# Two transformer-like blocks on one core: each feed-forward down projection as seven half-sized products instead of one full product

## The reference

```python
# first block (in the kernel: phase E)
h = rms_norm(x, norm_ffn_pre)
f = (silu(h @ w_ffn_gate) * (h @ w_ffn_up)) @ w_ffn_down      # [1024, 2816] @ [2816, 1024]
x = x + rms_norm(f, norm_ffn_post)
# second block (phase H); conv: depthwise, causal, width 3
g = rmsnorm(h, norm_ffn_g) @ w_up                             # [1024, 5632]
a, b = split(conv(g) + conv_b)
h = h + (silu(b) * a) @ w_down                                # [1024, 2816] @ [2816, 1024]
return rmsnorm(h, norm_final_g)
```

## Time and profile before

| | us |
|---|---|
| median of 3 runs | 3183.2 |
| lowest, highest | 3179.53, 3187.27 |
| the profiled execution | 3176.86 |
| its span in the trace | 3175.2 |
| PE matmuls busy | 2987.9 (94% of the span) |
| VectorE busy | 1918.5 (60%) |
| ScalarE busy | 1225.2 (39%) |
| GpSimd busy | 514.5 (16%) |

### The profile page before, as it was taken

How to read it: one execution, slowest core, us unless ns; L and a number is a source line. 1 busy time by engine, 2 the same in 40 slices (tenths; PEclk the granted TensorE clock), 3 DMA queues, 4 the chain that set the end, 5 groups by cost and what they waited for, 6 DMA issues and landing times.

```text
span 3175.2 us, 40775 instructions
## 1 busy us (share of the span) xinstructions
PE 2987.9 (94%) x15215; PEld 2443.7 (77%) x15215; DVE 1918.5 (60%) x2600; ACT 1225.2 (39%) x1900; POOL 514.5 (16%) x481
## 2 busy tenths in 40 slices
PE   8989999999989898999999998999988899999997
PEld 6767778778877676888878877788867677777886
DVE  3546565575675538555546675555745777776667
ACT  3531441542542445333322224556645444443212
POOL 3211121221221302222220001233410000000000
PEclk9999999999999999999999999999989999999999
DMA  4255356265242642222223234333244444443233
GB/s 141 67 165 141 119 130 180 82 147 162 89 116 68 225 138 80 80 79 82 86 85 128 96 115 139 103 121 115 86 144 139 119 116 116 117 116 120 93 106 119
DMA packets 268750, 370.81 MB, mean 117 GB/s; under 512 B 13346, under 2 KB 208688, under 8 KB 266048
## 3 DMA queue, kind: packets, MB, share of 16 engines
q1 hardware_dynamic: 240576, 261.45, 26.2%
q0 software_dynamic: 22224, 90.62, 10.4%
q10 hardware_dynamic: 5808, 16.79, 1.8%
HBM read 285.92 MB, written 129.03 MB: 131 GB/s over the span
## 4 chain that ended last, share of the span: by engine, by line
PE 72%; DVE 13%; ACT 5%; DMA 5%; issue 3%; POOL 1%; SPq 0%; DVEq 0%; ACTq 0%
PE PS L661 20%; PE PS L367 19%; PE PS L2373 17%; PE PS L1479 2%; DVE gate_up L2269 1%; PE PS L1373 1%; PE PS L1445 1%; PE PS L2978 1%; PE PS L1362 1%; DMA down_raw<-up_sums 1%; DMA sb_branch<-u_scratch 1%; PE PS L2965 1%; DVE silu_out L2249 1%; ACT silu_out L2101 1%; DVE w_L L2222 1%
## 5 line engine op out<-in xcount | busy, mean ns | idle before, releaser
L661 PE MATMUL PS<-hH,w_H 128*128 128x512 f32 x1072 | 452.2, 422 | 25.9 <-DVE w_L L324 13.0
L661 PE MATMUL PS<-hH,w_L 128*128 128x512 f32 x1072 | 425.1, 397 | 0.0
L661 PE MATMUL PS<-hL,w_H 128*128 128x512 f32 x1072 | 423.0, 395 | 0.0
L2189 DVE TENSOR_TENSOR ffn_sum<-ffn_sum,PS 128x1024 f32<-128x1024 f32 x160 | 195.4, 1221 | 139.3 <-PE PS L367 139.2
L324 DVE TENSOR_TENSOR w_L<-w_raw,w_H 128x1024 fp32r<-128x1024 f32 x107 | 133.8, 1251 | 216.7 <-ACT w_H L319 216.5
L661 PEld LDWEIGHTS PS<-hH,w_H 128*128 128x128 f32 x1072 | 206.2, 192 | 71.4 <-issue 12.1
L661 PEld LDWEIGHTS PS<-hH,w_L 128*128 128x128 f32 x1072 | 204.1, 190 | 46.3
L661 PEld LDWEIGHTS PS<-hL,w_H 128*128 128x128 f32 x1072 | 205.7, 192 | 35.6 <-issue 1.7
L2373 PE MATMUL PS<-hH,fast_w 128*128 128x512 f32 x672 | 227.3, 399 | 4.0 <-DVE fast_w L2222 3.9
L2373 PE MATMUL PS<-sums,w_H 128*128 128x512 f32 x672 | 212.5, 398 | 9.1 <-DVE gate_up L2269 8.4
L367 PE MATMUL PS<-hH 128*128 128x512 f32 x960 | 219.8, 390 | 0.0
(11 more groups left out here) (462 smaller groups left out, 6421.4 us busy)
## 6 DMA issues: line engine op xcount, KB each, us to landing
up_sums<-in_w_up POOLq DMA_DIRECT2D x24, 1408.0 KB, 10.9
w_raw<-in_w_in SPq DMA_DIRECT2D x62, 512.0 KB, 4.4
u_scratch<-unit_staged SPq DMA_DIRECT2D x50, 512.5 KB, 4.9
hidden_scratch<-hidden SPq DMA_DIRECT2D x42, 512.0 KB, 4.7
down_raw<-up_sums SPq DMA_DIRECT2D x42, 512.0 KB, 6.7
gate_up<-hidden_scratch SPq DMA_DIRECT2D x20, 1024.0 KB, 4.9
w_raw<-in_w_up SPq DMA_DIRECT2D x23, 512.0 KB, 4.0
...
```

The lines of the kernel that those rows point to most:

```text
L661: mm = e.matmul(PS[:, f.bank(o, half), :], w[:, k0 + k, :], x[:, k, half * HALF:(half + 1) * HALF], start=(k == 0 and j == 0), stop=(k == ...
L2189: e.tensor_tensor(yacc[:, b, :], yacc[:, b, :], bank2(4 + 2 * (b % 2)), ALU.add).then_inc(added, 1)
```

## The change

The down projection of both phases becomes seven products of halves, as in Strassen's scheme (Winograd's form). The 1024 tokens are halved, the 22 tiles are halved (tiles 0 to 10 and 11 to 21), and the 1024 output columns are halved. A step n = 11 q + i is tile i of product q: a 128x512 operand from the hidden side (a half of a hidden tile, or one of four sums of a pair of tiles), a 128x512 operand from the weight side (a quarter of the weights, or one of four sums), split as before, and 4 blocks x 3 passes = 12 matmuls. A product is accumulated over its 11 steps in PSUM (products 0 and 1 in the same banks, 2 to 4, 5 and 6). Its sum is read out once, by ScalarE for products 0 and 1 (`act_taken`), by VectorE for the others (`dve_taken`), which combines it with the other sums.

- All operands are streamed from DRAM: 2 x 256 KB a step, in four raw slots in turn, and nine slots for split operands.
- The four hidden sums of a pair of tiles are made by GpSimd in the tile loop (`pair_sums`), from the tile just computed and one loaded back, and stored. VectorE (E) or ScalarE (H) waits for them before it overwrites the hidden tile.
- The weight sums of both phases are made by 2 x 16 more accumulating DMAs on GpSimd's queue. E's 16 come first, then the 32 of before, then H's 16. B issues 3 + 5 + 5 for each pair of heads and 3 for the last, F one after every third step.
- The `keep_busy` transposes ahead of the down projection go.
- Blocks 0 to 3 are complete after product 4. Their epilogue is put between steps 60 to 75, at fixed step numbers on each engine; that of blocks 4 to 7 comes after the last step, all stages of a block in a written order.
- Some semaphores are merged with others (`dve_steps_B`, `inverse_started`, `F_dve_steps`), and tiles are laid out anew in SBUF; the order of the work is the same there.

```diff
+        DOWN_E_PARTS, UP2_PARTS, DOWN_H_PARTS = 16, 32, 16
+        def weight_sum_parts(e):
+            def part(dst, src, add):
+                if part.n:
+                    e.wait_ge(sem("weights_summed"), 16 * part.n)
+                e.dma_start(dst, src, accum_op=ALU.add if add else ALU.bypass, max_dma_last_dim=2 * DFF)\
+                    .then_inc(sem("weights_summed"), 16)
+                part.n += 1
+            part.n = 0
+            def down(t, w):
+                rows, half = NG * P, NG * P // 2
+                b11, b12, b21, b22 = (w[r * rows:(r + 1) * rows, c * HALF:(c + 1) * HALF] for r in range(2) for c in range(2))
+                for n, src, add in ((0, b11, False), (2, b12, False), (0, b12, True), (2, b22, True),
+                                    (1, t[0], False), (1, b22, True), (3, t[1], False), (3, b21, True)):
+                    for i in range(2):
+                        blk = slice(i * half, (i + 1) * half)
+                        part(t[n][blk], src[blk], add)
+                        yield
...
+            yield from down(down_sums[0], a["w_ffn_down"][0])
+            yield from gate_up(up2_sums, a["w_up_2"][0])
+            yield from down(down_sums[1], a["w_down_2"][0])
...
-                    sums(2)
+                    sums(3)
...
-                sums(2 if p == LAST else 4)
+                    e.memset(t[:, :, :], 0.0).then_inc(sem("inverse_started"), 1)
+                sums(3 if p == LAST else 5)
...
-                sums(4)
+                sums(5)
...
+        DOWN_A = ((HIDDEN, 0, 0), (HIDDEN, NG, 0), (SUMS, 1), (SUMS, 0), (SUMS, 3), (SUMS, 2), (HIDDEN, NG, 1))
+        DOWN_B = ((DOWN, 0, 0), (DOWN, NG, 0), (TSUM, 1), (TSUM, 0), (DOWN, NG, 1), (TSUM, 2), (TSUM, 3))
+        DOWN_BANK, DOWN_FIRST = (4, 4, 0, 0, 0, 4, 4), (0, 2, 5)
...
+        NSLOT = len(OP_SLOTS)
+        slot_no = lambda n: {ND - 2: 5, ND - 1: 6}.get(n, n % NSLOT)
...
+        raw_of = lambda n: RAW_SLOTS[n if n < 5 else 5 + (n - 5) % 4]
+        evac_after = lambda q: NG * q + NG - 1 + NSLOT - 1
...
+        def down_load(e, tag, n, w_down):
+            q, i = n // NG, n % NG
+            if n < 2:
+                e.wait_ge(sem("fast_L"), since(tag, "fast_L", 7 * NW - 1))
+            elif n in (3, 4):
+                e.wait_ge(sem("fast_P"), since(tag, "fast_P", 7 * (NW - 1) + 3))
+            elif n >= 5:
+                e.wait_ge(sem("fast_P"), since(tag, "fast_P", 7 * NW))
+            if n >= 4:
+                e.wait_ge(sem("down_L"), since(tag, "down_L", 2 * (n - 4) + 2))
+            if n == NG:
+                e.wait_ge(sem("fast_stored"), since(tag, "fast_stored", 16 * FT))
+            if n == 2 * NG:
+                e.wait_ge(sem("pair_stored"), since(tag, "pair_stored", 16 * NG))
+                e.wait_ge(sem("weights_summed"), 16 * (DOWN_E_PARTS if tag == "E" else
+                                                       DOWN_E_PARTS + UP2_PARTS + DOWN_H_PARTS))
...
+            s = sem(f"down_loaded{n % 4}")
+            for dst, src in zip(raw_of(n), (src_a, src_b)):
+                e.dma_start(dst, src).then_inc(s, 16)
...
+        def down_high(e, tag, n):
+            s = f"down_loaded{n % 4}"
+            e.wait_ge(sem(s), since(tag, s, 32 * (n // 4) + 32))
+            before = slot_before(n)
+            if before is not None:
+                down_used(e, tag, before)
+            elif n == 2:
+                e.wait_ge(sem("down_L"), since(tag, "down_L", 4))
+            elif n in (3, 4):
+                e.wait_ge(sem("fast_P"), since(tag, "fast_P", 7 * NW))
+            elif n == 5:
+                e.wait_ge(sem("hidden"), since(tag, "hidden", FT))
+            elif n == 6:
+                e.wait_ge(sem("fast_stored"), since(tag, "fast_stored", 16 * FT))
+                e.wait_ge(sem("pair_summed"), since(tag, "pair_summed", 8 * NG))
+            elif n == 7:
+                e.wait_ge(sem("pair_summed"), since(tag, "pair_summed", 8 * NG))
+                e.wait_ge(sem("down_L"), since(tag, "down_L", 6))
+            elif n == 8:
+                e.wait_ge(sem("pair_stored"), since(tag, "pair_stored", 16 * NG))
+            for i in range(2):
+                e.activation(OP_SLOTS[slot_no(n)][2 * i], raw_of(n)[i], ACT.Copy).then_inc(sem("down_H"), 1)
+        def down_low(e, tag, n):
+            for i in range(2):
+                high, low = OP_SLOTS[slot_no(n)][2 * i:2 * i + 2]
+                e.wait_ge(sem("down_H"), since(tag, "down_H", 2 * n + i + 1))
+                e.tensor_tensor(low, raw_of(n)[i], f32(high), ALU.subtract).then_inc(sem("down_L"), 1)
+        def act_taken(e, tag, q):
+            for b in range(4):
+                e.wait_ge(sem("y_part"), since(tag, "y_part", 4 * q + b + 1))
+                e.activation(yacc[:, b, lo if q else hi], PS[:, DOWN_BANK[q] + b, :], ACT.Copy).then_inc(sem("y_copied"), 1)
...
+            s = sem("y_added")
+            part, first, u = PS[:, DOWN_BANK[q] + b, :], yacc[:, b, hi], lambda n: since(tag, "y_added", n + b + 1)
+            e.wait_ge(sem("y_part"), since(tag, "y_part", 4 * q + b + 1))
+            if q <= 4:
+                e.wait_ge(sem("y_copied"), since(tag, "y_copied", b + 1))
...
+                out = (yacc[:, 4 + b, lo], yacc[:, 4 + b, hi], first)[q - 2]
+                e.tensor_tensor(out, part, first, ALU.subtract).then_inc(s, 1)
+            elif q == 5:
...
+            def pair_sums(it):
+                e.wait_ge(sem("hidden"), own("hidden", tag, 1, it, 1))
+                e.wait_ge(sem("pair_loaded"), own("pair_loaded", tag, -16 * NG + 16, it, 16))
+                if not (isinstance(it, int) and it == NG):
+                    e.wait_ge(sem("pair_stored"), own("pair_stored", tag, -16 * NG, it, 16))
+                summed = sem("pair_summed")
+                done = lambda n: e.wait_ge(summed, own("pair_summed", tag, n, it, 4))
+                s1, s2, s3, s4 = (pair_sum[:, i, :] for i in range(4))
+                e.tensor_tensor(s1, pair_h[:, hi], hfE[:, hi], ALU.subtract).then_inc(summed, 1)
+                done(1)
+                e.tensor_tensor(s2, pair_h[:, lo], s1, ALU.subtract).then_inc(summed, 1)
+                done(2)
+                e.tensor_tensor(s4, hfE[:, lo], s2, ALU.subtract).then_inc(summed, 1)
+                e.tensor_tensor(s3, pair_h[:, lo], pair_h[:, hi], ALU.subtract).then_inc(summed, 1)
+                done(4)
+                e.sem_inc(s_held, 1)
+                one = (lambda x: bass.ds(it - NG, 1)) if not isinstance(it, int) else (lambda x: slice(it - NG, it - NG + 1))
+                e.dma_start(pair_scr[:, :, one(0), :].rearrange("n p o c -> p n o c"),
+                            pair_sum[:, :, :].rearrange("p n (o c) -> p n o c", o=1)).then_inc(sem("pair_stored"), 16)
+            def pair_load(it):
+                one = bass.ds(it - NG + 1, 1) if not isinstance(it, int) else slice(it - NG + 1, it - NG + 2)
+                e.dma_start(pair_h[:, :].rearrange("p (o t) -> p o t", o=1), h_scr[:, one, :]).then_inc(sem("pair_loaded"), 16)
+            e.sem_inc(sem("pair_summed"), 4 * NG)
             weight_sums(0, None)
-            def turn(it, following):
-                if following:
-                    weight_sums(1, it)
             if tag != "H":
-                ffn_tiles(e, turn)
+                weight_sums(1, None)
+                with e.Fori(1, NG) as i:
+                    weight_sums(1, i)
+            e.wait_ge(sem("hidden"), since(tag, "hidden", 2))
+            pair_load(NG - 1)
+            weight_sums(1, NG)
+            pair_sums(NG)
+            pair_load(NG)
+            with e.Fori(NG + 1, NW - 1) as i:
+                weight_sums(1, i)
+                pair_sums(i)
+                pair_load(i)
+            pair_sums(NW - 1)
+            pair_load(NW - 1)
+            pair_sums(NW)
...
+            for n in range(3, ND):
+                down_high(e, tag, n)
+                for q in range(2):
+                    if n == evac_after(q):
+                        act_taken(e, tag, q)
+                between(n)
...
+                    for n in range(3):
+                        down_low(e, tag, n)
...
+            for n in range(5, ND):
+                down_low(e, tag, n)
+                for q in range(2, 6):
+                    if n == evac_after(q):
+                        for b in range(4):
+                            dve_taken(e, tag, q, b)
+                between(n)
...
+            def part(n, b):
+                q, i = n // NG, n % NG
                 if b == 0:
-                    e.wait_ge(sem("down_L"), since(tag, "down_L", 2 * i + 2))
-                    if i == 0:
-                        keep_busy(e, 4, 30 if conv else 16)
-                    e.wait_ge(sem("hidden_L"), since(tag, "hidden_L", 2 * i + 2))
-                if 8 * i + b >= 2:
-                    e.wait_ge(sem("y_added"), since(tag, "y_added", 8 * i + b - 1))
-                s = i % 2
-                for kt in range(2):
```

(65 more changed lines are left out.)

351 lines of the change are left out of this document (207 added, 144 removed).

## The result

The changed kernel takes 3210.66 us (median), the kernel before 3181.36 us beside it on the same chip: ratio 1.0088, 95% interval 1.0071 to 1.0106. It is slower, by 0.9%; 3138 us was forecast, with a range that ended at 3168. One of the six runs of the changed kernel took 9518 us and is left out of the ratio (the median of the other five is 3208.11). The profiled execution has a span of 3211.7 us against 3175.2.

The account below looks back on a forecast made before the run. TensorE's matmuls, 72% of the chain that ended last, were taken as the bound. Gains of 35.6 (E) and 30.1 us (H), less 15, 2 and 4, gave 44.7 us: median 3183.2 to 3138 us, range 3116 to 3168.

Parts of the forecast that it names:

- products, start and end of E: First FFN's down projection: fewer products gain 30.0 us, an earlier start 3.1, the end 2.5; 35.6 us in all.
- products, start and end of H: Second FFN's down projection: fewer products gain 30.0 us, an earlier start 2.5, the end loses 2.4; 30.1 us in all.
- pair sums in H's loop: H's tile loop: GpSimd's adds slow two or three VectorE differences a tile; 1.5 us x 10 tiles = 15 us lost.
- weight sums in B: Stage B: more DRAM sums on GpSimd's queue, mostly covered by idle time; 2 us lost (0 to 10).
- weight sums in F: Stage F: 22 issues on GpSimd's queue, mostly covered by three probability buffers; 4 us lost (0 to 20).
- so 0 there: E's tile loop: VectorE idles 3.07 us before the next tile's sum, so the pair sums cost 0 us.
- rival 4: Down projections: operand landings of 10.2 us make a step 3.4 us, 100 us lost, 3238 us; chance 0.06.
- I count about 0.5 us of PE wait at each: Down projections, changes of product 2 to 3, 3 to 4, 5 to 6: VectorE's late reads cost 1.7 us per FFN.
- rival 3: Stages B and F: GpSimd's queue becomes late, 20 us more together, 3158 us; chance 0.10.
- the pitch: Down projections: time per matmul, length over count, taken to stay at 0.2272 us.
- the gap in H before the pair operands: Start of H's down projection: a gap of 2 to 5 us near step 5 or 6.
- rival 2: H's tile loop: pair sums cost whole GpSimd instructions, 43 us in place of 15, 3166 us; chance 0.11.

Follow-up runs that it names:

- split_evac: The changed kernel with GpSimd doing pair adds, weight sums, then the pair's store and load, and ScalarE copying the first two products earlier: 3160.02 us, ratio 0.9938.
- pair_no_traffic: The changed kernel with the pair sums' adds kept but their store and load cut to 16 columns: 3177.06 us, ratio 0.9992.

## Why the prediction was wrong

By its own terms, forecast and measured change in us:

```
                                  forecast   after    split_evac
products, start and end of E       -35.6     -18.8     -31.0
products, start and end of H       -30.1     -18.5     -31.0
pair sums in E's loop                0       +34.8      +6.3
pair sums in H's loop              +15       +10.7      +9.5
weight sums in B (A to D)           +2        +4.8      +3.5
weight sums in F                    +4       +21.9     +21.8
G                                    0        +1.6      +0.9
sum                                -44.7     +36.5     -20.1 (rounded)
```

1. **The step that failed first** is "so 0 there" for the pair sums in E. It asked only whether VectorE had idle time under a slower difference, and for that alone it was nearly right (pair_no_traffic: 3 us), with luck in it: the 3.07 us of idle time that it cites lie at the tile's start, and the adds fall behind the weight sums, where VectorE of the kernel before has gaps of 0.17 and 0.86 us. It never placed the pair's store and load in the tile, nor the adds behind the weight sums on GpSimd. Three facts that could be known beforehand (GpSimd's order, 1.5 MB on its queue, the weight load at the tile's start) close to a ring that costs 34.8 us: the weights land in 9.0 us in place of 5.2, and a tile takes 23.8 us where 19.6 was forecast. No rival held it: rival 4 spoke of transfers, but in the down projection.
2. **"I count about 0.5 us of PE wait at each"** counted VectorE's reads of finished sums and overlooked ScalarE's. The copy of product 0 is put behind step 18, and the steps up to it are late at the start of the stream: 12.45 and 11.05 us of idle time, and some 2 us of slower matmuls behind each. VectorE's reads cost 3.25 us in E, at the seventh product.
3. **Weight sums in F, 4 us (0 to 20)**: the range priced GpSimd's queue (rival 3). The cost was another one: the parts' traffic on the landings of F's own small transfers (256 and 512 KB), at most 5.8 us on the chain before and up to 12.5 now. 21.9 us lie just outside the range. The queue's cost came out as soon as the parts were put closer.
4. **Right**: the pitch (0.2284 to 0.2289 us; rival 4's bound of 3.4 us a step was not reached, at a DMA share of 0.62 and a median landing of 3.1 us where 4.8 was taken; only steps 10 to 13 had landings up to 11.6 us, over its 8.8, and these stand behind item 2); the first down matmul 0.6 us behind E's loop and 3.2 us behind H's (0.7 and 3.4 forecast); the gap in H before the pair operands, spread over 1.31, 1.45 and 0.71 us; the end of H, 16.2 us from the last matmul to the end (18.9). In E the last three down matmuls wait 6.11 us for a turned block, and 19.7 us pass from their end to the last turned block; counted from where the matmuls would have ended without that wait it is some 28 us (an estimate; 30.9 forecast). In split_evac H's rest falls by 31.0 us (30.1 forecast), E's by 31.0 (35.6 forecast: 2.18 us for ScalarE's copy, 3.25 for VectorE's read, and slower matmuls are left).
5. **Pair sums in H**: the mechanism was right, 15 us was 10.7; rival 2's 43 us did not come. Two differences a tile were held up, not three, by 0.85 and 1.08 us, and the tile grew by 1.0 us of these 1.9. That each ended 0.55 us behind an add of GpSimd fits the exclusive port in the Trainium skill, "SBUF — State Buffer" (section "SBUF: two separate sides"), where the later of the two waits for the other's whole instruction; a difference pays only what is left of the add.
6. **Weight sums in B, 2 us**: 4.8 measured, and 4.7 in the kernel before profiled once more, so no run here shows this term.

What stays open: how much of F's cost is the traffic's amount and how much the kind of the parts (accumulating, 2 KB rows on GpSimd's queue); the 4 us of F that stay without parts; and the 5 us in A to D.
